# A two-model transformer kernel: its first norm scale loaded as one row and spread by TensorE, VectorE casts the first half slab, second tile turned inside the first unit

## The reference

```
for l in range(2):
    h = rmsnorm(x, pre_g[l])                      # x * rsqrt(mean(x*x) + 1e-6) * pre_g[l]
    proj = h @ w_in[l]                            # 1024 x 2816
    u_a, v_a, g_a, q, k, v, g_b = split(proj)
    y = concat(gmlp(u_a, v_a) * silu(g_a), attention(q, k, v) * silu(g_b))
    x = x + rmsnorm(y @ w_out[l], post_g[l])
```

## Time and profile before

| | us |
|---|---|
| median of 3 runs | 988.0 (987.45 to 988.04) |
| the profiled execution, its own time | 987.43 |
| its span in the profile | 985.6 |
| PE busy | 965.1, 98% of the span |
| DVE busy | 634.9, 64% |
| ACT busy | 494.8, 50% |
| POOL busy | 254.5, 26% |

### The profile page before, as it was taken

The page is one execution under the profiler, slowest core; times in us unless marked ns, Lnnn a source line. Parts: engine busy times, 40 slices in busy tenths (PEclk is TensorE's granted clock), DMA queues, the critical chain, the costliest instruction groups (busy, mean ns, idle before and its releaser), DMA issues.

```text
span 985.6 us, 13708 instructions
## 1 busy us (share of the span) xinstructions
PE 965.1 (98%) x4934; PEld 815.5 (83%) x4934; DVE 634.9 (64%) x943; ACT 494.8 (50%) x904; POOL 254.5 (26%) x203
## 2 busy tenths in 40 slices
PE   7999999999999999999999899999999999999997
PEld 6988888888888888888788788888888887888885
DVE  5677777938687687846535788599556986312214
ACT  5445656624435656725348677523557983222222
POOL 2216200003126200003231010240324885224231
PEclk9999999999999999999999999999999999999999
DMA  8332201232422301133332002122220112323312
GB/s 288 110 117 68 86 22 44 80 114 68 141 86 86 107 22 44 44 128 81 108 106 90 19 1 86 43 86 86 86 87 21 44 44 69 103 86 107 129 43 85
DMA packets 66791, 80.45 MB, mean 82 GB/s; under 512 B 5520, under 2 KB 50704, under 8 KB 66720
## 3 DMA queue, kind: packets, MB, share of 16 engines
q1 hardware_dynamic: 64816, 76.64, 24.5%
q10 hardware_dynamic: 1904, 2.88, 0.9%
HBM read 77.42 MB, written 2.10 MB: 81 GB/s over the span
## 4 chain that ended last, share of the span: by engine, by line
PE 60%; issue 28%; ACT 5%; DVE 3%; POOL 3%; DMA 1%; POOLq 0%; ACTq 0%; DVEq 0%
PE ps L1924 16%; PE ps L1926 16%; PE ps L1925 15%; PE ps L1979 1%; PE ps L1981 1%; PE ps L1980 1%; PE ps L2279 1%; PE ps L2409 1%; PE ps L2424 1%; ACT whi L947 1%; DMA x<-in_x 1%; POOL small L553 1%; PE ps L2437 1%; ACT qsb L953 1%; PE ps L2299 1%
## 5 line engine op out<-in xcount | busy, mean ns | idle before, releaser
L598 POOL TENSOR_TENSOR wlo<-raw,whi 128x2048 fp32r<-128x2048 f32 (+1 forms) x22 | 96.4, 4384 | 189.5 <-ACT whi L947 179.7
L1924 PE MATMUL ps<-whi,hhi 128*128 128x512 f32 (+1 forms) x320 | 115.9, 362 | 1.5 <-DVE hlo L1256 0.8
L1924 PE MATMUL ps<-hhi,whi 128*128 128x512 f32 x288 | 113.6, 394 | 1.4 <-ACT sp L1044 1.4
L1926 PE MATMUL ps<-whi,hlo 128*128 128x512 f32 (+1 forms) x320 | 114.5, 358 | 0.0
L1925 PE MATMUL ps<-wlo,hhi 128*128 128x512 f32 (+1 forms) x320 | 114.4, 358 | 0.0
L1926 PE MATMUL ps<-hhi,wlo 128*128 128x512 f32 x288 | 112.3, 390 | 0.0
L1925 PE MATMUL ps<-hlo,whi 128*128 128x512 f32 x288 | 112.3, 390 | 0.0
L947 ACT ACTIVATE whi<-raw 128x2048 fp32r<-128x2048 f32 (+1 forms) x30 | 54.9, 1828 | 86.9 <-PE ps L1926 86.8
L1265 DVE TENSOR_TENSOR wlo<-raw,whi 128x2048 fp32r<-128x2048 f32 (+1 forms) x29 | 63.6, 2191 | 39.3 <-ACT whi L713 38.0
L713 ACT ACTIVATE whi<-raw 128x2048 fp32r<-128x2048 f32 (+1 forms) x29 | 52.2, 1799 | 72.9 <-PE ps L1926 72.9
L1979 PE MATMUL ps<-hhi,whi 128*128 128x512 f32 x192 | 76.8, 400 | 0.0
(11 more groups left out here) (322 smaller groups left out, 2342.5 us busy)
## 6 DMA issues: line engine op xcount, KB each, us to landing
raw<-in_w_in SPq DMA_DIRECT2D x42, 1024.0 KB, 5.3
raw<-in_w_out SPq DMA_DIRECT2D x12, 1024.0 KB, 5.1
raw<-in_w_in SPq DMA_DIRECT2D x10, 512.0 KB, 3.9
raw<-in_w_branch_swa SPq DMA_DIRECT2D x4, 1024.0 KB, 4.9
raw<-in_w_branch_sb SPq DMA_DIRECT2D x4, 512.0 KB, 3.5
x<-in_x ACTq DMA_DIRECT2D x3, 512.0 KB, 6.6
out<-x SPq DMA_DIRECT2D x3, 512.0 KB, 2.6
ws<-in_spatial_w SPq DMA_DIRECT2D x2, 512.0 KB, 6.7
```

The lines of the kernel that those rows point to most:

```text
L598: pool.tensor_tensor(wlo[s][:, 0:n, :], raw[s][:, 0:n, :], whi[s][:, 0:n, :].bitcast(F32), ALU.subtract).then_inc(slab_split, 1)
L1924: pe.matmul(out_ap, lhsT=lhi(k), rhs=rhi(k), start=first and k == 0, stop=False, skip_group_check=True)
L1926: m = pe.matmul(out_ap, lhsT=llo(k), rhs=rhi(k), start=False, stop=last and k == n - 1, skip_group_check=True)
```

## The change

It does six things, all in the head of the program but the last.

1. The first norm scale is loaded as one row of 4 KB into partition 0 of `row_gain` (`first_gain`), in place of the 512 KB copy to all partitions. POOL fills a row of 128 ones (`ones_row`, one more memset). TensorE multiplies the column of ones by the row in two float32 matmuls of 512 columns, which puts the scale into all partitions of PSUM banks 6 and 7 (`gain_spread`).
2. DVE's four `normalise` of layer 0 become `first_normalise`: they wait for `gain_spread` and read the scale from PSUM.
3. DVE, not ACT, casts piece 0 of slab 0 to `whi`.
4. ACT casts slab 1 before it copies the transposed tile 1, not after. DVE's order is interleaved to fit.
5. TensorE transposes tile 1 between the first six and the last six matmuls of unit (0, 0), and the identity transposes that fill waits go from 16, 10 and 5 to 8 and 5.
6. Unit (0, 0) becomes a function `first_unit`. It stands ahead of the loop for layer 0, and for the next layer (and the second model) at the end of the loop body, without a transposition inside it.

```diff
         tri, tri_rest, ident_r = (consts_r[:, 128 * i:128 * i + 128] for i in range(3))
         mask_sb, mask_sw, mask_sw0 = consts_r[:, 384:512], consts_r[:, 384:640], consts_r[:, 640:784]
         ones_meta, tri_meta = consts_r[:, 784:1024], consts_r[:, 1024:1152]
+        first_gain, ones_row = row_gain[0:1, :], small[0:1, 128:256]
         ss = small[:, 0:4]
         post_rs, norm_rs, half_mean = small[:, 88:92], small[:, 92:96], small[:, 96:100]
         vn_rs = small[:, 100:104]
...
             pool.sem_inc(slab_split, RING)
             pool.memset(eps_tile, EPS).then_inc(pool_const, 1)
             pool.memset(minus_half, -0.5).then_inc(pool_const, 1)
-            pool.wait_ge(pool_const, 2)
+            pool.memset(ones_row, 1.0).then_inc(pool_const, 1)
+            pool.wait_ge(pool_const, 3)
 
             def x_root(l, ahead, t, steps):
 
...
         @block.scalar
         def _(act):
             act.dma_start(x[:, 0, 512:], a["x"][0, 0:P, 512:]).then_inc(x_loaded[0], 16)
-            act.dma_start(norm_gain[:], rows_to_all(a["norm_gains"], 0, D)).then_inc(norm_loaded, 16)
+            act.dma_start(first_gain, bass.AP(a["norm_gains"].tensor, 0, [[D, 1], [1, D]])).then_inc(norm_loaded, 16)
             def split_hi(l, i):
 
                 n = i % SLABS
...
             act.wait_ge(x_loaded[1], 16)
             sum_x(0, 0, 1)
             load_x(2)
-            first_slab_hi(0, 0, 0)
+            first_slab_hi(0, 0, 1)
             load_x(3)
             transposed_x(0, 0, 0)
-            first_slab_hi(0, 0, 1)
             act.dma_start(rope[:], a["rope1"].rearrange("c (t p) d -> p c t d", p=P)).then_inc(rope_loaded, 16)
+            split_hi(0, 1)
             transposed_x(0, 0, 1)
-            split_hi(0, 1)
             for t in (2, 3):
                 act.wait_ge(x_loaded[t], 16)
                 sum_x(0, 0, t)
...
             FIRST = 0
 
             dve.sem_inc(x_back, 4)
-            normalise(0, 0, 0)
-            normalise(0, 0, 1)
+
+            def first_normalise(t):
+
+                dve.wait_ge(gain_spread, 1)
+                dve.wait_ge(norm_root, t + 1)
+                dve.scalar_tensor_tensor(xs[:, t, :].rearrange("p (b n) -> p b n", b=2),
+                                         x[:, t, :].rearrange("p (b n) -> p b n", b=2), norm_rs[:, t:t + 1],
+                                         ps[:, F_BANK:F_BANK + 2, :], ALU.mult, ALU.mult).then_inc(xs_ready, 1)
+
+            first_normalise(0)
+            dve.wait_ge(first_loaded, 16)
+            dve.tensor_copy(whi[0][:, 0:4, :], raw[0][:, 0:4, :]).then_inc(first_hi, 1)
             first_slab_low(0, 0, 0)
             transposed_x(0, 0, 0, (0,))
+            first_normalise(1)
             first_slab_low(0, 0, 1)
             transposed_x(0, 0, 0, (1,))
-            transposed_x(0, 0, 1)
+            transposed_x(0, 0, 1, (0,))
             slab_low(0, 1)
-            normalise(0, 0, 2)
-            normalise(0, 0, 3)
+            transposed_x(0, 0, 1, (1,))
+            first_normalise(2)
+            first_normalise(3)
             transposed_x(0, 0, 2)
             with dve.Fori(0, DEPTH) as l:
                 transposed_x(l, 0, 3)
...
                     m.then_inc(tr_done, 1)
 
             pe.sem_inc(unit_done, CREDIT)
+            pe.wait_ge(pool_const, 3)
+            pe.wait_ge(norm_loaded, 16)
+            for half in range(2):
+                m = pe.matmul(ps[:, F_BANK + half, :], lhsT=ones_row, rhs=first_gain[:, 512 * half:512 * half + 512],
+                              start=True, stop=True)
+            m.then_inc(gain_spread, 1)
             pe.wait_ge(const_loaded, 16)
-            for n in range(16):
-                pe.matmul(ps[:, F_BANK, 0:P], lhsT=ident[:], rhs=ident[:], is_transpose=True)
+            for n in range(8):
+                pe.matmul(ps[:, F_BANK - 1, 0:P], lhsT=ident[:], rhs=ident[:], is_transpose=True)
             x_transposed(0, 0, 0)
-            for n in range(10):
-                pe.matmul(ps[:, F_BANK, 0:P], lhsT=ident[:], rhs=ident[:], is_transpose=True)
-            x_transposed(0, 0, 1)
             for n in range(5):
-                pe.matmul(ps[:, F_BANK, 0:P], lhsT=ident[:], rhs=ident[:], is_transpose=True)
+                pe.matmul(ps[:, F_BANK - 1, 0:P], lhsT=ident[:], rhs=ident[:], is_transpose=True)
+
+            def first_unit(l, ahead, turned_between=None):
+
+                hi, lo = wide(whi[0]), wide(wlo[0])
+                pe.wait_ge(h_ready, l * 8 + ahead * 8 + 1)
+                for at_ in (0, 2):
+                    if at_ and turned_between is not None:
+                        x_transposed(l, ahead, turned_between)
+                    pe.wait_ge(*((slab_split, l * SLABS + ahead * SLABS + RING + 1) if at_
+                                 else (first_low, l + ahead + 1)))
+                    m = product(ps[:, 0, :], lambda k: hhi[:, at_ + k, 0:P], lambda k: hlo[:, at_ + k, 0:P],
+                                lambda k: hi[:, at_ + k, :], lambda k: lo[:, at_ + k, :], 2, first=at_ == 0, last=False)
+                m.then_inc(unit_done, 1)
+
+            first_unit(0, 0, 1)
             with pe.Fori(0, DEPTH) as l:
                 def slab_here(i):
                     pe.wait_ge(slab_split, l * SLABS + RING + i + 1)
...
                     hi, lo = wide(whi[s]), wide(wlo[s])
                     m = None
                     for at_ in (0, 2):
-                        if (i, t) == (0, 0):
-                            pe.wait_ge(*((slab_split, l * SLABS + RING + 1) if at_ else (first_low, l + 1)))
                         m = product(ps[:, t, :], lambda k: hhi[:, 4 * half + at_ + k, t * P:t * P + P],
                                     lambda k: hlo[:, 4 * half + at_ + k, t * P:t * P + P], lambda k: hi[:, at_ + k, :],
                                     lambda k: lo[:, at_ + k, :], 2, first=half == 0 and at_ == 0,
...
                         m.then_inc(unit_done, 1)
 
 
-                for n, (i, t) in enumerate(FIRST_UNITS):
+                for n, (i, t) in enumerate(FIRST_UNITS[1:], 1):
                     if n in TILE_AT:
                         x_transposed(l, 0, TILE_AT[n])
                     if (i, t) == (1, 0):
```

6 lines of the change are left out of this document (3 added, 3 removed).

## The result

The changed kernel took 993.46 us as the median of six executions, from 989.01 to 995.02, against 988.02 (987.45 to 989.43) for the kernel before in six beside them. The ratio is 1.0045, 95% interval [1.0033, 1.0057]. I had forecast 987.7 with a range up to 989.0, so this is a miss, and on the side to which I had given 0.06.

A forecast was written before the change was run, and what follows sets the result against it. PE was taken to bound the kernel. First matmul from 13.95 to 12.2, less 0.6 at the branch and 0.9 waiting for DVE, leaves 0.3 us at the second unit: 988.0 - 0.3 = 987.7 us, 80% range 986.5 to 989.0.

The forecast's parts named there:

- the side to which I had given 0.06: Whole kernel: a time beyond 990.0 us, from a low clock or the worst of a late spread; chance 0.06.
- the one costed at nothing: Unit (0, 0) at the loop's end: same matmuls and waits, no cost; unhidden register work under 0.1 us per pass.
- The spread: Head, PE's two float32 matmuls of the scale row: four passes each, 3.6 us together, ending at 8.3.
- The row: Head, DMA of the scale row: lands at 4.7 us, with ends of 4.2 and 6.6.
- Tile 1 of x: Head, DMA: without the 512 KB copy, put at 1.3 us, tile 1 lands at 7.3 instead of 8.6.
- The first product: Head, PE: first useful matmul at about 12.2 us against 13.95, with DVE's subtraction, not ACT's copies, as the later.
- The second six: Head, last six matmuls of unit (0, 0): wait for DVE's second subtraction until 14.35, run from 14.5 to 15.9.
- The branch into the loop: Head, PE's entry into the loop behind unit (0, 0): 0.58 us more from start to start than usual.
- The second unit: End of the head on PE: starts at 16.5 us instead of 16.79, gaining 0.3 us.
- The last rival: Head: clock still low in the first unit, at 1.2 GHz until 16 us; about +2.2 us, 990.2; chance 0.04.
- a late spread: Head: row queued or passes reload weights, delaying the second unit; 989.6, likelier 988.9 us; chance 0.15.
- nothing there would soak up a shift: PE after the head: every wait hangs on PE's earlier units, so a shift moves the end by the same amount.

The follow-up runs named there:

- the long execution: One profiled execution of the changed kernel, with no edit, that took 996.78 us.
- after_again: The changed kernel run once more as it is: median 988.56 us, ratio 1.0021 to the kernel before.
- after_12: The changed kernel with twelve identity transposes, not five, between tile 0's transposes and the first unit: 988.60 us, ratio 1.0007.
- branch_between: The changed kernel with PE's loop branch between the two groups of six matmuls of unit (0, 0): 988.33 us, ratio 1.0015.
- before_few: The kernel before with its fillers cut from 16, 10 and 5 to 8, 0 and 5: 989.03 us, ratio 1.0015.
- unit_in_loop: The changed kernel with unit (0, 0) back inside the loop and tile 1 transposed ahead of it: 990.33 us, ratio 1.0020.
- after_0: The changed kernel with no filler between tile 0's transposes and the first unit: 991.78 us, ratio 1.0029.
- after_pad: The changed kernel with 14 increments of a spare semaphore ahead of TensorE's first matmul: 989.33 us, ratio 1.0008.
- after_warm: The changed kernel with thirteen matmuls of a zeroed tile ahead of the spread and twelve fillers, not five, behind tile 0: 988.51 us, ratio 1.0004.
- move_alone: The kernel before with only unit (0, 0) moved ahead of the loop and to its body's end: 987.71 us, ratio 1.0001.
- move_few: The kernel before with only unit (0, 0) moved and 16 of its 31 spare transposes cut: 990.32 us, ratio 1.0026.
- after_12_flat: The changed kernel with twelve fillers, not five, before the first unit and PE's layer loop written out: 988.32 us, ratio 1.0004.

## Why the prediction was wrong

**The step that failed** is the one costed at nothing: "The move of unit (0, 0) to the loop's end keeps the same matmuls with the same waits; the branch's 0.43 us of idle now follow the unit in place of going before it." The 0.43 us were not the price of the branch. The taken branch lasted 3.59 us, and 0.43 was what 3.44 us of queued matmuls had left of it. I took over a remainder as a price. At its new place the branch begins 3.8 us later (238.05 for 234.24), its load with it (239.09 for 235.22), and over the profiles with the moved unit only 2.0 to 2.3 us of matmuls cover it. The idle is 1.2 to 1.9 us with one load and 2.9 to 3.2 with two. The unit isn't "the same matmuls with the same waits" as far as the branch goes: ahead of it there now stand the two waits of the unit, for hlo and for the second piece's wlo. DVE finished that subtraction at 237.90, and the branch's record begins 0.15 us behind it. In the long execution the two are at 238.44 and 238.76, in after_again at 238.19 and 238.50, in after_12 at 238.61 and 238.78. In branch_between, where only the wait for the first hlo stands ahead of the branch, it begins at 237.25, behind DVE's 237.01, and there too only 2.03 us cover it.

The transfer of the weights is not needed for this. With no such transfer under way the branch took 3.3 to 3.6 us (before, before_few, unit_in_loop), and inside it with one load 3.3 to 4.1. The load makes up 0.9 to 1.6 of that, 0.8 to 1.0 us passes ahead of it, and the next product starts 1.5 to 1.8 us behind its end. What makes it two loads in some executions stays open.

The Trainium skill, "Advanced Engine Details and Errata", section "Control Flow Timing", gives about 108 ns for a compare-and-branch. By that figure the branch would have been free at either place. The runs agree only for the branch that falls through, 83 ns. The taken one took 3.3 to 5.2 us, with the load of its target, which that line doesn't count.

**How 1 to 3 us of gap become up to 9.** In short executions the waits that the kernel before has at 250.30 and 254.73 take it up: in the quickest profile the unit behind the gap starts 1.14 us later than before, the transposes at 251.28 are 0.98 late, and the unit at 254.92 is 0.19 late. In long ones two things follow. First, the clock: in 4 of the 6 profiles with a gap of 1.93 us or more it fell for 3.4 us, the fall beginning from 0.5 us before the end of the gap (after_0) to 1.4 us behind it, 1.7 us lost each time. In none of those with 1.70 or less did it fall there. That is no threshold: four of these profiles have another wait of 1.3 to 1.9 us between 257 and 260 us, and no fall behind it, while behind the wait of 1.63 us for DVE at 562.86 it fell in four profiles of twenty. Second, ACT and DVE have loops and branches of their own, ACT's between its copies of tile 2 and tile 3 and DVE's between its hlo of the same tiles, and these are pushed into the next slab's transfer. The quickest profile of the changed kernel and then the long one, ACT's copies and SP's request for the slab:

```profile
248.30 1.09 ACT L732 ACTIVATE hhi<-ps 128x512 fp32r<-128x512 f32 x2 [0.30 <-PE ps L1948]
252.69 1.09 ACT L732 ACTIVATE hhi<-ps 128x512 fp32r<-128x512 f32 x2 [3.30 <-PE ps L1948]
...
250.43 0.38 SPq L462 DMA_DIRECT2D raw<-in_w_in  x1
```

```profile
251.72 1.09 ACT L732 ACTIVATE hhi<-ps 128x512 fp32r<-128x512 f32 x2 [3.16 <-PE ps L1948]
259.61 1.08 ACT L732 ACTIVATE hhi<-ps 128x512 fp32r<-128x512 f32 x2 [6.80 <-issue]
...
250.98 0.38 SPq L462 DMA_DIRECT2D raw<-in_w_in  x1
```

SP's request hangs on DVE, not on PE, and comes at 250.43 and 250.98. With PE late, ACT reaches its branch behind it: at 252.22, where it was at 248.81 in the first. The next instruction load on the queue that ACT and DVE seem to share is at 250.89 in the first, 2.0 us behind ACT's branch, and at 257.07 in the second, 4.8 us behind it. ACT stands still for 6.80 us with nothing awaited, hlo comes late, and PE waits 2.48 us at 260.98. In the first profile ACT also went on only 3.7 us behind its branch, but PE's transposes had ended just before and its next units did not wait. From the start of the copies to the request it is 2.1 us in the first and -0.7 in the second. Over eleven profiles of the changed kernel, after_12, branch_between, after_0 and after_pad, PE's wait goes with it: none at 2.1 to 2.3, 0.59 at 0.96, 1.55 at 0.67, 1.31 at 0.27, 1.7 to 2.5 below zero. Left out here are after_warm, move_alone and move_few, which have 2.3 us and waits of 0.2 to 0.3 all the same, as the kernel before has 0.59 at 2.3. So the tie is one for the longer waits. This was read from traces and not tried: neither ACT's nor DVE's loop was written out in any run, so it is argued and not shown.

**The other steps.** *The spread*: 3.6 us forecast, 3.75 measured, four records for two instructions. The four passes that I weighed from the Trainium skill, "FP8 and Floating Point Precision", section "TensorE Precision Notes", agree with it now. *The row* landed at 4.16 and not 4.7, so DVE began at 7.95, 0.45 earlier than forecast. *Tile 1 of x* I had at 7.3; ACT's second sum began at 8.58, for 8.64 in the earlier trace rows. Taking 508 KB out of the queue gave 0.06 us in this execution. Over the seven profiles the sum began at 8.58 to 9.14 five times and at 7.17 and 7.16 in the other two (990.34 and 991.84 us). So the term of 1.3 us was right in two and nothing in five, and I had it for all. *The first product* came at 12.95 for a forecast of 12.2: tile 0's transposes ran at the lower level (1.83 us for eight), ACT's cast of piece 1, which waited for its DMA, ran from 10.63 and held the copies until 11.60, and DVE waited 0.98 us for them; I had it the other way round. In the two profiles with the early sum the cast ran from 9.1, and the product came at 12.23 and 12.05. *The second six*: 15.28 for 14.5. *The branch into the loop*, 0.58 by my sum, cost nothing: the second unit followed the twelfth matmul by 0.23. *The second unit*: 16.77 for 16.5. *The last rival*, a low clock in the first unit: the clock had risen by 13.6 us in each profile of the changed kernel, in the profiled one at 11.2, with only the spread and transposes run by then. In the kernel before it rose at 10.4 with transposes alone. This is against the rule of the Trainium skill, "TensorE: Matmul & The Clock Gate", Part 4, that transposes don't count.

That the second unit's mean of 16.74 is close to the forecast of 16.5 is partly luck, since the row was early, the first product late and the branch into the loop free. My bet on the sign was on a late spread at 0.15, a cause in the head. The loss lies 225 us away from all that I costed. I had written that after the head "nothing there would soak up a shift". That was wrong too: in the quickest profile the waits at 250 and 254 us took up 0.95 us of the 1.14, which is why the profiled execution looked harmless.

**What stays open.** Why after_pad has three executions above 991 and after_12, with the same loop end, has none in eleven (a difference that chance can give). Whether the second load is the block behind the loop's end, and why it comes in some executions only. How much the chip matters, since most kernels ran on one chip each. Whether writing out the loops of ACT and DVE as well would take the rest away. No run beats the kernel before by more than can be measured.

## What to carry to other kernels

An idle gap at a loop's branch is only the part that other work doesn't cover: before a branch is moved, read the branch's own record, when it begins and how long it lasts, which waits will stand ahead of it at its new place, and how many microseconds of queued work will cover it there. Do so for the loops of the other engines too. When one profile agrees with the forecast and the median doesn't, take more profiles before explaining anything: here the trace that came with the result was the quickest of six, and its largest difference was noise that the kernel before has as well. And a wait that is usually absorbed still costs, if the clock can fall behind it.

## What the runs showed of the hardware that I had not expected

A float32 matmul of one row against 512 columns took 1.9 us (3.75 for two) at the clock's lower level. In after_warm PE was busy from 1.28 us on with a zeroed tile, the spread, fillers and transposes, and the clock rose only at 12.1.

The same pause doesn't always have the same effect. Behind the wait of about 1.6 us at 563 the clock fell in four profiles of twenty (and in about a quarter of the executions of the kernel before, as I read their times), and behind gaps near 3 us in three of five. The Trainium skill, "TensorE: Matmul & The Clock Gate", Part 1, calls the window in which activity is counted free-running. These counts would fit that, and don't test it.

A taken branch of a loop took TensorE's sequencer 3.3 to 4.1 us with one load of 16 KB and 4.9 to 5.2 with two, and the same branch 0.08 us when it fell through. Two instruction loads at once took 1.2 to 2.3 us each beside the slab's transfer, where one alone took 0.9 to 1.6.

One execution of after_12_flat, out of some 280 in this study, took 1964.25 us, about twice the usual. It has no profile. TensorE at half its clock throughout would explain such a time. But its recorded mean clock is 1.000, so the record shows no fall. That fits only if the clock never rose, since the low level ahead of the first rise leaves no record in any profile here. The cause is open.
